# Down projection of a hybrid encoder layer on Trainium2: its first output tile waits for each of its 22 input tiles instead of for all of them at once

## The reference

```python
hf = rms_norm(x, g_ffn)
x = x + (jax.nn.silu(hf @ w_gate) * (hf @ w_up)) @ w_down
...
y_prompt = rms_norm(xp, g_final)
y_sample = rms_norm(xs, g_final)
```

## Time and profile before

| | |
|---|---|
| median of 3 runs | 932.15 us |
| lowest, highest | 932.09, 936.19 us |
| the profiled execution's own time | 937.43 us |
| its span, first to last instruction | 935.6 us |
| mean granted TensorE clock in it | 0.973 |
| TensorE busy with matmuls | 888.7 us, 95% of the span |
| VectorE, ScalarE, GpSimd busy | 40%, 37%, 39% |
| share of TensorE in the chain that ended last | 71% |
| DMA traffic | 75.45 MB, mean 81 GB/s |

### The profile page before, as it was taken

How to read it: one execution, slowest core, us unless ns; L and a number is a source line. 1 busy time by engine, 2 the same in 40 slices (tenths; PEclk the granted TensorE clock), 3 DMA queues, 4 the chain that set the end, 5 groups by cost and what they waited for, 6 DMA issues and landing times.

```text
span 935.6 us, 15437 instructions
## 1 busy us (share of the span) xinstructions
PE 888.7 (95%) x6170; PEld 825.0 (88%) x6170; DVE 376.2 (40%) x579; ACT 348.1 (37%) x602; POOL 366.8 (39%) x184
## 2 busy tenths in 40 slices
PE   6999999989999999898898999999999998999994
PEld 6988987667877899887698999999999998999994
DVE  6255464656557656734383222222222220211203
ACT  6343554545656424444352323233232231211210
POOL 5344853544225445632052443443333442333310
PEclk9999999899999999899999999999999998999997
DMA  7333421100013333330032323223223222222202
GB/s 234 113 100 104 144 60 42 35 18 24 23 69 124 113 111 110 91 95 23 1 93 77 87 83 90 87 70 90 71 86 90 83 68 63 85 79 85 85 18 102
DMA packets 25091, 75.45 MB, mean 81 GB/s; under 512 B 2880, under 2 KB 5000, under 8 KB 24904
## 3 DMA queue, kind: packets, MB, share of 16 engines
q1 hardware_dynamic: 25040, 74.74, 26.3%
HBM read 68.20 MB, written 6.53 MB: 80 GB/s over the span
## 4 chain that ended last, share of the span: by engine, by line
PE 71%; DVE 5%; issue 3%; ACT 2%; POOL 1%; DMA 0%; DVEq 0%; ACTq 0%
PE ps L368 21%; PE ps L369 20%; PE ps L370 20%; PE ps L532 3%; PE ps L516 1%; PE ps L768 1%; PE ps L386 1%; DVE sqacc L1534 1%; PE ps L394 1%; DVE xb L1657 1%; DVE hlo L1527 1%; POOL wlo L1668 1%; PE ps L538 0%; DMA wraw<-w_ff 0%; PE ps L501 0%
## 5 line engine op out<-in xcount | busy, mean ns | idle before, releaser
L368 PE MATMUL ps<-hhi,whi 128*128 128x288 f32 x1120 | 337.2, 301 | 16.6 <-POOL wlo L1668 9.1
L369 PE MATMUL ps<-hhi,wlo 128*128 128x288 f32 x1120 | 333.8, 298 | 0.0
L370 PE MATMUL ps<-hlo,whi 128*128 128x288 f32 x1120 | 333.4, 298 | 0.0
L1786 POOL TENSOR_TENSOR wlo<-wraw,whi 128x1024 fp32r<-128x1024 f32 (+1 forms) x68 | 161.3, 2372 | 268.5 <-ACT whi L868 268.5
L368 PEld LDWEIGHTS ps<-hhi,whi 128*128 128x128 f32 x1120 | 214.2, 191 | 19.6 <-POOL wlo L1668 9.1
L369 PEld LDWEIGHTS ps<-hhi,wlo 128*128 128x128 f32 x1120 | 212.6, 190 | 0.1
L370 PEld LDWEIGHTS ps<-hlo,whi 128*128 128x128 f32 x1120 | 212.6, 190 | 0.0
L1668 POOL TENSOR_TENSOR wlo<-wraw,whi 128x1024 fp32r<-128x1024 f32 (+1 forms) x49 | 117.8, 2409 | 221.8 <-ACT whi L868 212.7
L868 ACT ACTIVATE whi<-wraw 128x1024 fp32r<-128x1024 f32 (+1 forms) x117 | 119.1, 1023 | 142.3 <-PE ps L370 129.3
L368 PE MATMUL ps<-hidhi,whi 128*128 128x288 f32 x352 | 105.4, 299 | 3.4 <-DVE hidlo L1643 3.4
L369 PE MATMUL ps<-hidhi,wlo 128*128 128x288 f32 x352 | 105.3, 299 | 0.0
(11 more groups left out here) (227 smaller groups left out, 1326.8 us busy)
## 6 DMA issues: line engine op xcount, KB each, us to landing
wraw<-w_ff SPq DMA_DIRECT2D x44, 512.0 KB, 3.5
wraw<-w_front SPq DMA_DIRECT2D x41, 512.0 KB, 3.6
wraw<-w_down SPq DMA_DIRECT2D x16, 512.0 KB, 3.6
wraw<-w_front SPq DMA_DIRECT2D x8, 384.0 KB, 3.7
wraw<-w_down SPq DMA_DIRECT2D x8, 384.0 KB, 3.2
xs<-x_t SPq DMA_DIRECT2D x8, 288.0 KB, 6.0
xa<-x_t SPq DMA_DIRECT2D x8, 288.0 KB, 5.0
out_y<-xb SPq DMA_DIRECT2D x8, 288.0 KB, 2.3
```

Of the source, the lines that this page charges most:

```text
L368: nc.tensor.matmul(out, lh, rh, start=start, stop=False)
L369: nc.tensor.matmul(out, ll, rh, start=False, stop=False)
L370: return nc.tensor.matmul(out, lh, rl, start=False, stop=stop)
L1786: g.tensor_tensor(ffw(c, 1, 1, n)[:, 0, :], wraw[:, c % 2, 0:n], f(ffw(c, 0, 1, n)[:, 0, :]), ALU.subtract)\
```

## The change

The three waits in front of the down stage go. Output tile 0 now waits for `s_gr` to reach 21 (PSUM pair 0 has been read for hidden tile 20), output tile 1 for `s_hf` to reach 21 (the same for pair 1), and output tiles 2 to 7 for `r_x` as before. `wide` of output tile 0 gets a `wait_k` that waits in front of the six matmuls of input tile k until `s_hidlo` says that this hidden tile is complete. For the other output tiles the function does nothing.

```diff
-            pe.wait_ge(s_hidlo, FT)
-            pe.wait_ge(s_gr, FT)
-            pe.wait_ge(s_hf, FT)
             for m in range(KT):
                 if m >= 2:
                     pe.wait_ge(r_x, 16 + m - 1)
+                else:
+                    pe.wait_ge(s_hf if m else s_gr, FT - 1)
                 for c, kn in enumerate(DOWN_K):
                     g = 2 * FT + 3 * m + c
                     pe.wait_ge(g_lo, g + 1)
                     wide(m % 2, kn, lambda k: [ffw(g, lo, kn, 128)[:, k, :] for lo in (0, 1)], (hidhi, hidlo), c == 0, c == 2,
-                         sum(DOWN_K[:c])).then_inc(g_used, 1)
+                         sum(DOWN_K[:c]), lambda k: pe.wait_ge(s_hidlo, sum(DOWN_K[:c]) + k + 1) if m == 0 else None)\
+                        .then_inc(g_used, 1)
```

## The result

The changed kernel takes 925.78 us (median of 4 runs, 924.33 to 927.00) where the kernel before took 932.12 (4 runs, 931.32 to 936.19): ratio 0.9913, 95% interval 0.9889 to 0.9938. A second comparison with more runs gave 926.58 (6 runs) against 932.81 (17 runs), ratio 0.9938, interval 0.9922 to 0.9954, which is 5.8 us with bounds of 4.3 and 7.3. The forecast was 925.8 and a gain of 6.4.

A forecast was written before the change was run, and what follows sets the result against it. TensorE, busy 95% of the span, was taken to bound the kernel, so an edit pays only where it idles or clocks lower. 3.60 + 2.79 - 0 - 0 = 6.4 us off the median 932.15 gave 925.8 us, range 922.6 to 929.0.

The forecast's parts named there:

- Stand-still: Between the last up and first down product TensorE stands idle for the last hidden tile; removing this gains 3.60 us.
- Low clock: At the down stage's start the granted clock falls to 0.50 after the idle time; avoiding this gains 2.79 us.
- Waits: The 22 waits in output tile 0 of the down stage cost 0 us, with 2.2 us as upper bound.
- Nothing late next: In the down stage PSUM pairs, hidden tiles and weight blocks are all ready before their products need them.
- Tail: The tail after the down stage moves earlier but is not changed: 0 us, at most 1.6 us of gain.
- From profile to median: The whole down stage sets the end, so the profile's 6.4 us comes off the timed median 932.15 unchanged.
- Waits that cost 0.10 each: Each of the 22 down-stage waits breaks the product stream, 0.10 us each: gain 4.2, time 928.0; chance 0.07.
- the slower case: Down-stage waits cost over 0.50 us each, making it slower by over 0.5%; at 0.55, 937.9 us; chance 0.04.
- no effect: TensorE still stands still at the down stage because something else is late: 932.2 us; chance 0.06.
- The stand-still alone: Only the idle time before the down stage comes back, 3.6 us, the clock falling anyway: 928.5 us; chance 0.10.

The follow-up runs named there:

- experiments 4: The changed kernel, also waiting in front of the down stage for both PSUM reads of hidden tile 21: 927.68 us, ratio 0.9946.
- experiment 5: The changed kernel, also waiting in front of the down stage for the high parts of all 22 hidden tiles: 930.81 us, ratio 0.9972.
- experiment 1: The kernel before, all waits kept, with 24 extra thrown-away products issued while the last hidden tile is finished: 929.19 us, ratio 0.9965.
- Experiment 2: The changed kernel with three waits in front of every input tile's six products in all 8 output tiles: 928.19 us, ratio 0.9949.

## Why the prediction was right

- **Stand-still, 3.60 us.** Right to the hundredth. The first down product comes 0.13 us after the last up product, and the profiles of experiments 4 and 5 have 1.06 and 2.61 us of it again. The timed runs confirm experiment 5; 1.1 us is too little for them.
- **Low clock, 2.79 us.** Right, and for the reason given: experiment 1 brings back 2.69 of it without touching the stand-still. The other 0.10 is not the clock but the first step behind a stop, which experiment 1 still has. The prediction knew this cost from the earlier trace rows and counted it under the low clock; the sum is the same, since the change removes both.
- **Why 2.8 and not 3.4.** By the Trainium skill ("TensorE: Matmul & The Clock Gate", section "Terms") the low clock would cost half of the stretch, an estimate of 3.4 us; the two profiles decide for 2.8. The prediction laid the difference to the 0.76 us in which TensorE was idle, but half of the busy 6.07 us is still 3.04. The rest is that a step at the low level takes (782.14 - 776.86) / 22 = 0.24 us, which is 1.8 times 0.1333 and not twice:

```profile
776.86 0.44 PE L369 MATMUL ps<-hidhi,wlo 128*128 128x288 f32 x1
...
782.14 0.44 PE L370 MATMUL ps<-hidlo,whi 128*128 128x288 f32 x1
```

- **Waits, 0 us.** Right. Experiment 2 has 24 times as many and the same 140.63 us. The 50 to 100 ns for a semaphore read in the Trainium skill ("Advanced Engine Details and Errata", section "Network/Comms") do not reach the products of this stage.
- **Nothing late next.** Right: block 47 had 11.6 us to spare, as forecast, and hidden tile 21 was ready 3.6 us after the stage began, 13 us before its products.
- **Tail, 0 us.** Too low for the profiled pair, where it gave 1.0, within the bounds of 0 and 1.6. The 2.30 us of the columns stand in the one profile of before alone; experiment 1, which is before with extra products elsewhere, has 1.28. Whether the timed runs of before paid for it no trace shows, so this term stays untested.
- **From profile to median.** 6.4 us were taken off the median as they stood. The timed gains are 5.8 and, in the first comparison, 8.1 by the ratio; 6.4 lies in both intervals. That the median of the first comparison met the forecast to 0.02 us is luck; the second is 0.8 higher. The step held because the timed runs lose the low clock here as the profiled one did: the 7.1 us less at the low level show it, on average and not run by run. The stated range began at 922.6, whereas the forecast's own range and its working begin at 922.3; nothing hangs on it.
- **Rivals.** Waits that cost 0.10 each and the slower case fall with experiment 2; "no effect" falls with the timeline. The stand-still alone (928.5) falls with experiment 1; the times alone would hardly have told it, as 4.3 us, the low bound of the second comparison, is near its 3.6. The argument against it in the prediction was weaker than it looks: a digit of the clock line covers 23.4 us, and the stretch of 3.4 us at 495.80 lies in the stage under a digit 9. (The stage lasts 288 us, from 484.49 to 772.72, not 264.) The window of before from the end of that stretch to the fall carries the argument:

```profile
499.20:775.69 276.49, 272.97 (x2046) 1.00 0.28 81
```

## What to carry to other kernels

Look for the place where a stage waits for the whole of its input although its first products need only the oldest part, and count the producer's last chain plus the low clock behind the idle time, here 3.6 + 2.8 us. Waits that are already met cost nothing here on TensorE, even three of them for every 0.8 us of products, and a coarse one placed behind enough other work does as well as many fine ones. Where a stand-still can't be removed, products that are thrown away can still save the clock behind it, if ready operands and a PSUM bank that holds nothing needed are at hand.

## What the runs showed of the hardware

- Throw-away products in front of a wait made the kernel faster: 929.19 against 932.77 us with 24 of them in one place.
- A step between products took 0.24 us at 1.2 GHz and 0.1333 at 2.4 GHz, and the first step behind a stop at full clock took 0.21 to 0.24 us (experiments 1, 4 and 5).
- At this place the clock held through 1.06 and 2.61 us of stand-still in one profile each and fell 2.68 us into one of 3.60. Elsewhere it is not regular: the stretch of 10.2 us from 390 is in the profile of the changed kernel, but not in that of its second comparison.
- The time at the low level differed from run to run of one kernel between 28 and 51 us, and a straight line on it takes up 87% of the variance of the 41 runs of before.
